# Moving sixteen modulation units into the projection stage, and reordering the attention side work, in a two-block transformer kernel

## The chip, the cores and the metric

The kernel runs on one core of one Trainium2 chip. The time is the device time in microseconds (us) of one launch. Three runs of the kernel before gave 1226.17, 1227.54 and 1229.17 us, median 1227.54 us.

TensorE (PE) multiplies, VectorE (DVE) and ScalarE (ACT) do elementwise work, GpSimd (POOL) computes a few powers, and SyncE (SP) issues most DMAs. Each engine works through its own instruction list in order and waits on semaphores for the others.

## The reference, cut to what matters

One sequence of 256 tokens of width 1024 goes through two blocks, all in fp32.

```python
# block 1
mods = silu(c) @ w_ada + b_ada            # 9 vectors of 1024: shift, scale, gate for 3 sublayers
n = modulate(rmsnorm(h, g_pre0), shift0, scale0);  f = swiglu(n, gate, up, down)   # ffn0
h = h + 0.5 * gate0 * rmsnorm(f, g_post0)
n = modulate(rmsnorm(h, g_pre1), shift1, scale1);  p = n @ w_in
oa = rmsnorm(dsa_sparse_attention(...))   # 8 heads, top 64 keys by an index score, softmax
ob = rmsnorm(stick_breaking_attention(...))   # 8 heads
h = h + gate1 * rmsnorm(concat(oa, ob) @ w_out, g_post1)
n = modulate(rmsnorm(h, g_pre2), shift2, scale2);  f = swiglu(...)                 # ffn1
h = h + 0.5 * gate2 * rmsnorm(f, g_post2)
# block 2
h = h + diff_attention(rms_norm(h), w_qkv, w_o, ...)   # rope on q and k, two softmaxes a head
h = h + sq_relu_mlp(...);  h = h + mla_attention(...);  h = h + sq_relu_mlp(...)
return rms_norm(h)
```

`mods` holds nine vectors, numbered 0 to 8. Vectors 0 and 1 are wanted by ffn0, 2 by the residual after it, 3 and 4 by the projection `w_in`, 5 by the residual after `w_out`, 6 and 7 by ffn1, and 8 by the residual after that.

## The kernel before, in words

**The stream.** All weights lie in DRAM as one stream of units, each 128 x 1024 fp32 (512 KB), in the order that `stream_plan` writes (line 67). SP loads them two at a time (a chunk of 1 MB) into a ring of five chunks, `raw`. `feed` (line 338) takes the units in order. A weight unit is split into two parts that add up to it: ACT copies the high part (`whi`, L354) and DVE subtracts it (`wlo`, L355), into one of five slots, so that PE can multiply with three passes (high x high, high x low, low x high, L392). An "ada" unit is no weight for PE: DVE multiplies it by `silu(c)` and sums it into one column of `mods` (L333), and eight ada units make one of the nine vectors. `spread` (line 69) mixes ada units among weight units; its last argument sets how densely.

**ffn0.** It has 22 blocks of 128 hidden columns. Eight are made while the first modulation vectors arrive, the other 14 pairs (gate, up) and 22 down units follow, 50 weight units, and 48 ada units (vectors 2 to 7) are spread among them. Beside them `constants_and_table` (line 905) advances one step with each pair or down unit: ACT writes a small row table to DRAM (`bias_rows`) and loads it back shifted, 1 MB (`arena<-bias_rows`), and PE flips it in four matmuls (L405), two of them first. `modulations` turns finished vectors into columns and gate rows.

**The projection with attention beside it.** After `in_v` (8 units) and `in_i`, 20 `in_t` units in `IN_ORDER` make the transposed queries and keys. A `Side` object (line 175) runs generators between them: its clock `now` goes up by one with each `nudge`, half way and at the end of each unit, and a part that yields n is resumed n nudges later (2 if it yields nothing). `index_part` scores and picks keys (L1061, L1063 on DVE), `stick_head` and `sparse_head` are the heads. A stick head is: scores on PE; ACT Abs, Exp, Ln and DVE L1108; yield 3; cumulative sums on PE ("second product"), ACT, DVE L1116, ACT L1118; yield 3; times values on PE. A sparse head is: scores; DVE L1084 and L1015, ACT exponentials L1020, DVE L1089; yield 3; transpose (PE L993, ACT L996); yield; times values and DVE L1026. `half_out` normalises eight finished heads (ACT L1175, POOL, DVE L519) and `mixed` multiplies them by the diagonal (PE L1186) into four chunks (ACT L1191, DVE L1192). These are the input of the `out` units, 8 of them in `OUT_ORDER` (chunks 4 to 7 first).

**Differential attention.** 16 `qk` units are projected (q and k in turn). Each needs a rope: ACT L1265 copies, PE L405 turns it, DVE L1270 and L1274 or L1276 add. `rope_end`, put at the head of the side's list by `soon`, does the PE and DVE half at the next nudge, which is half way through the next unit. `diff_head` is the head's generator (DVE L1015, L1320 to L1328, L1342).

## Time and profile before

| what | value |
|---|---|
| median of three runs | 1227.54 us (1226.17 to 1229.17) |
| the profiled execution's own time | 1227.54 us |
| its span | 1226.2 us, mean granted clock 0.985 |
| PE busy | 1171.4 us (96%) |
| DVE busy | 796.8 us (65%) |
| ACT busy | 618.6 us (50%) |
| stream loads on SP | 213 chunks of 1 MB |

The busy share of PE says that some 55 us of the span at most are idle, but it counts a slow matmul as busy too. TensorE's granted clock is 1.00 (2.4 GHz) in most of the span and 0.50 (1.2 GHz) in a few stretches of some 6 us. So time can be lost in two ways, as idle time and as work at half the clock.

### The profile page before, as it was taken

What the parts mean: (1) busy time and instruction counts of PE and PEld (TensorE: products, weight loads), DVE (VectorE), ACT (ScalarE), POOL (GpSimd) and SP (SyncE); (2) the same over time, 40 slices, a digit from 0 to 9 for tenths busy, and PEclk for the clock granted to TensorE, in tenths of its full rate; (3) what the DMA queues carried; (4) which work ended last, traced back from release to release, by engine and by line L of the source; (5) the groups of instructions that cost most, each with busy time, mean ns of one, the idle gap of its engine ahead of it and who ended that gap; (6) DMA issues with size and microseconds to landing.
All of it is one profiled execution on the core that took longest, in us unless ns stands there. A gap on an engine that the chain in (4) does not pass through costs nothing.

```text
span 1226.2 us, 19544 instructions
## 1 busy us (share of the span) xinstructions
PE 1171.4 (96%) x7742; PEld 1074.6 (88%) x7742; DVE 796.8 (65%) x1310; ACT 618.6 (50%) x1114; POOL 55.8 (5%) x75
## 2 busy tenths in 40 slices
PE   4999999999988999999999899999999889999998
PEld 4988799899977999999989788999998778899997
DVE  4879788758654666565667776555557665655554
ACT  5644343646654644444545455554546545555453
POOL 3100000000000000000002110000000100000000
PEclk9999899999998999999999989999999999999999
DMA  8969999443222365654343223545454414554540
GB/s 348 401 261 415 352 344 348 154 180 138 104 98 75 124 240 207 224 218 172 138 176 138 83 104 127 200 175 197 181 190 151 175 35 154 175 200 176 194 150 35
DMA packets 34010, 231.78 MB, mean 189 GB/s; under 512 B 3704, under 2 KB 5120, under 8 KB 6528
## 3 DMA queue, kind: packets, MB, share of 16 engines
q1 hardware_dynamic: 31952, 226.24, 49.9%
q10 hardware_dynamic: 1968, 4.29, 1.0%
q8 instruction: 62, 1.02, 0.3%
q14 instruction: 28, 0.23, 0.1%
HBM read 229.45 MB, written 1.06 MB: 188 GB/s over the span
## 4 chain that ended last, share of the span: by engine, by line
PE 78%; DVE 11%; ACT 5%; issue 2%; DMA 2%; POOL 1%; ACTq 0%; DVEq 0%; SPq 0%; POOLq 0%
PE ps L392 35%; PE pacc L392 34%; DVE wlo L355 3%; PE ps L402 2%; PE ps L405 2%; ACT wk L1020 2%; PE pacc L402 2%; DVE raw L333 1%; DMA raw<-in_stream 1%; ACT whi L354 1%; POOL st L499 1%; PE ps L531 1%; PE pacc L531 1%; DVE st L1015 1%; DVE tmp L668 1%
## 5 line engine op out<-in xcount | busy, mean ns | idle before, releaser
L355 DVE TENSOR_TENSOR wlo<-raw,whi 128x1024 fp32r<-128x1024 f32 x353 | 430.6, 1226 | 194.8 <-ACT whi L354 188.0
L354 ACT ACTIVATE whi<-raw 128x1024 fp32r<-128x1024 f32 x353 | 368.4, 1054 | 164.8 <-PE pacc L392 84.2
L392 PE MATMUL ps<-nhi,whi 128*128 128x256 f32 x1272 | 368.3, 290 | 1.8 <-DVE arena L1270 1.0
L392 PE MATMUL ps<-nlo,whi 128*128 128x256 f32 x1272 | 361.9, 284 | 0.0
L392 PE MATMUL ps<-nhi,wlo 128*128 128x256 f32 x1272 | 361.7, 284 | 0.0
L392 PEld LDWEIGHTS ps<-nhi,whi 128*128 128x128 f32 x1272 | 245.9, 193 | 7.3 <-DVE arena L1270 1.3
L392 PEld LDWEIGHTS ps<-nlo,whi 128*128 128x128 f32 x1272 | 245.9, 193 | 4.9 <-issue 0.8
L392 PEld LDWEIGHTS ps<-nhi,wlo 128*128 128x128 f32 x1272 | 245.7, 193 | 0.0
L743 ACT ACTIVATE sg<-ps 128x256 f32<-128x256 f32 x104 | 39.8, 383 | 164.5 <-PE ps L392 164.3
L392 PE MATMUL pacc<-whi,mhi 128*128 128x512 f32 x240 | 96.5, 402 | 2.4 <-DVE mlo L1192 2.4
L392 PE MATMUL pacc<-wlo,mhi 128*128 128x512 f32 x240 | 94.5, 394 | 0.0
L392 PE MATMUL pacc<-whi,mlo 128*128 128x512 f32 x240 | 93.9, 391 | 0.0
L745 DVE TENSOR_TENSOR hm<-sg,ps 128x256 f32<-128x256 f32 x104 | 43.7, 421 | 69.8 <-ACT sg L743 69.7
L333 DVE SCALAR_TENSOR_TENSOR raw<-raw,silu_c 128x1024 f32<-128x1024 f32 x72 | 88.2, 1233 | 0.3 <-DMA raw<-in_stream 0.3
L392 PE MATMUL pacc<-whi,hhi 128*128 128x512 f32 x188 | 74.4, 396 | 1.8 <-ACT sg L743 1.1
L392 PE MATMUL pacc<-wlo,hhi 128*128 128x512 f32 x188 | 73.6, 392 | 0.0
L392 PE MATMUL pacc<-whi,hlo 128*128 128x512 f32 x188 | 73.2, 389 | 0.0
L499 POOL TENSOR_TENSOR st<-st,mod 128x1 f32<-128x1 f32 (+1 forms) x40 | 26.9, 672 | 1015.7 <-DVE st L689 421.8
L392 PEld LDWEIGHTS pacc<-whi,mhi 128*128 128x128 f32 x240 | 45.7, 190 | 10.9 <-ACT hhi L1191 2.6
L392 PEld LDWEIGHTS pacc<-whi,mlo 128*128 128x128 f32 x240 | 45.4, 189 | 10.1
L392 PEld LDWEIGHTS pacc<-wlo,mhi 128*128 128x128 f32 x240 | 45.7, 191 | 7.8 <-issue 0.5
L392 PE MATMUL pacc<-whi,nhi 128*128 128x512 f32 (+1 forms) x128 | 50.0, 391 | 0.9 <-DVE n2lo L557 0.5
(305 smaller groups left out, 1784.8 us busy)
## 6 DMA issues: line engine op xcount, KB each, us to landing
raw<-in_stream SPq DMA_DIRECT2D x213, 1024.0 KB, 4.9
gates<-in_g_post ACTq DMA_DIRECT2D x3, 512.0 KB, 6.4
h<-in_x SPq DMA_DIRECT2D x1, 1024.0 KB, 7.0
cst<-in_const ACTq DMA_DIRECT2D x1, 1024.0 KB, 4.8
arena<-bias_rows ACTq DMA_DIRECT2D x1, 1024.0 KB, 18.8
out<-tmp SPq DMA_DIRECT2D x4, 256.0 KB, 2.1
silu_c<-in_c_row ACTq DMA_DIRECT2D x1, 512.0 KB, 5.9
arena<-in_final_g SPq DMA_DIRECT2D x1, 512.0 KB, 5.7
```

What stands on the lines that cost most here:

```text
L333: t = dve.do(lambda e: e.scalar_tensor_tensor(src, src, 1.0, silu_c[:, :], ALU.mult, ALU.mult, accum_out=adac[:, 8 * m + k:8 * m + k + 1]) ...
L354: t_hi = act.do(lambda e: e.activation(whi[:, s, :], src, ACT.Copy), arrived, room)
L355: t_lo = dve.do(lambda e: e.tensor_tensor(wlo[:, s, :], src, whi[:, s, :].bitcast(F32), ALU.subtract), arrived, room, t_hi)
L392: return e.matmul(o, lt[a], rh[b], start=start and first, stop=stop and last)
L402: pe.quiet(lambda e: e.matmul(o, lt, rh, start=start, stop=stop), *after)
L405: return pe.do(lambda e: e.matmul(o, lt, rh, start=start, stop=True), *after)
L499: return pool.do(lambda e: e.tensor_tensor(r, v, ex, ALU.pow), t, t_zero)
L531: tok[c] = pe.do(lambda e: e.matmul(o, a, dg[:, i, :], start=True, stop=True), t, held[c].free)
L668: t = dve.do(lambda e: e.scalar_tensor_tensor(tmp[:, i, w], fix[2 * i + f].ap, r1[i], gates[:, slot, w], ALU.mult, ALU.mult), t1[i], t_gate)
L743: t = act.do(lambda e: e.activation(sg[:, m, :], up if gate is None else gate, ACT.Relu if gate is None else ACT.Silu), tk)
L745: t = dve.do(lambda e: e.tensor_tensor(hm[:, m, :], sg[:, m, :], up, ALU.mult), t)
L1020: toks.append(act.do(lambda e: e.activation(dst.ap[:, a:a + w], src[:, a:a + w], ACT.Exp, bias=mx[:, i:i + 1], accum_out=sm[:, i:i + 1]), ...
```

## The change

1. **The stream.** Vectors 6 and 7 (16 ada units) leave ffn0's stretch and are spread among the last ten `in_t` units and the first four `out` units. The 32 units that stay in ffn0 are spread with 1.1 in place of 1.03.
2. **The side work of the projection.** `sparse_head` waits two nudges in place of three between its softmax and its transposes. The sparse heads stand ahead of both `half_out` parts in the list of waiting work. `mixed` is a generator that yields between its four chunks.
3. **Differential attention.** A unit's rope is finished at the end of the next unit, not half way through it, and a head starts three nudges after its k rope or later. `soon` goes.

```diff
-    plan += spread(ffn("ffn0_", DFF // P, ("gate", "up"), 8), (2, 3, 4, 5, 6, 7), 1.03)
+    plan += spread(ffn("ffn0_", DFF // P, ("gate", "up"), 8), (2, 3, 4, 5), 1.1)
     plan += [("in_v", k) for k in range(8)] + [("in_i", 0)]
-    plan += [("in_t", j) for j in IN_ORDER]
-    plan += [("out", k) for k in OUT_ORDER]
+    plan += [("in_t", j) for j in IN_ORDER[0:10]]
+    plan += spread([("in_t", j) for j in IN_ORDER[10:]] + [("out", k) for k in OUT_ORDER[0:4]], (6, 7), 1.2)
+    plan += [("out", k) for k in OUT_ORDER[4:]]
...
-    def soon(self, part):
-
-        self.active.insert(0, (self.now + 1, part))
...
             t_rs = dve.do(lambda e: e.reciprocal(rs, sm), t_e)
-            yield 3
+            yield
             pt, t = transpose_p(lg, t_e)
...
         def mixed(a, chunk, ts):
             for c in range(4):
+                if c:
+                    yield 1
                 b = banks.take()
...
             yield 3
-            mixed(a, chunk, ts)
-            yield
+            yield from mixed(a, chunk, ts)
...
+        for hh in range(8):
+            side.add(sparse_head(hh), lambda hh=hh: ripe(hh // 2, 4 + hh // 2) and sel_at and side.now >= sel_at[0] + 3)
         side.add(half_out(512, 4, t_b, 4096), lambda: len(t_b) == 8 and len(t_sel) == 2)
         side.add(half_out(0, 0, t_a, 5120), lambda: len(t_a) == 8 and 7 in o1.t)
-        for hh in range(8):
-            side.add(sparse_head(hh), lambda hh=hh: ripe(hh // 2, 4 + hh // 2) and sel_at and side.now >= sel_at[0] + 3)
...
-            side.add(diff_head(hh), lambda hh=hh: ripe(hh, 8 + hh))
-
-        def rope_end(at, rope):
-            t_q[at], born[at] = next(rope), side.now
-            yield
-
+            side.add(diff_head(hh), lambda hh=hh: ripe(hh, 8 + hh) and side.now - born[8 + hh] >= 3)
+        pend = None
         for hh in range(8):
             for g in (0, 8):
...
                 next(rope)
+                if pend is not None:
+                    t_q[pend[0]], born[pend[0]] = next(pend[1]), side.now
+                pend = (g + hh, rope)
                 feed()
                 side.nudge()
-                side.soon(rope_end(g + hh, rope))
+
+        def last_rope(at, rope):
+            t_q[at], born[at] = next(rope), side.now
+            yield
+
+        side.add(last_rope(*pend))
```

What stands on the engines follows from the plan and the side's clock. The changed kernel's line numbers are three lower from line 197 to `mixed`, so that L355 before is L352 after and L333 is L330; from `mixed` to the sparse heads' place they are one lower.

On DVE in ffn0, behind the eighth block that was made ahead: the last rows before the ninth block's `hm` (L745), before the change.

```order
L355 TENSOR_TENSOR wlo<-raw,whi 128x1024
L333 SCALAR_TENSOR_TENSOR raw,adac<-raw,silu_c 128x1024
L355 TENSOR_TENSOR wlo<-raw,whi 128x1024
L333 SCALAR_TENSOR_TENSOR raw,adac<-raw,silu_c 128x1024
L745 TENSOR_TENSOR hm<-sg,ps 128x256
```

The same place after it.

```order
L352 TENSOR_TENSOR wlo<-raw,whi 128x1024
L330 SCALAR_TENSOR_TENSOR raw,adac<-raw,silu_c 128x1024
L352 TENSOR_TENSOR wlo<-raw,whi 128x1024 x2
L330 SCALAR_TENSOR_TENSOR raw,adac<-raw,silu_c 128x1024
L742 TENSOR_TENSOR hm<-sg,ps 128x256
```

Five weights and five ada units stand ahead of that `hm` before, five weights and three ada units after; ahead of the tenth `hm` stand four and four more before, four and three after.

On DVE in the projection stage, around the first two stick heads' L1116 (`wk<-wk,pacc`), with the key selection (L1061, L1063) between, before.

```order
L974 TENSOR_SCALAR arena<-ps 64x256
L355 TENSOR_TENSOR wlo<-raw,whi 128x1024
L1116 TENSOR_TENSOR wk<-wk,pacc 128x384
L1061 MAX st<-hm 128x8 x2
L1063 MATCH_REPLACE hm<-st,hm 128x128
L1063 MATCH_REPLACE hm<-st,hm 128x256
L1116 TENSOR_TENSOR wk<-wk,pacc 128x384
```

After.

```order
L971 TENSOR_SCALAR arena<-ps 64x256
L352 TENSOR_TENSOR wlo<-raw,whi 128x1024
L330 SCALAR_TENSOR_TENSOR raw,adac<-raw,silu_c 128x1024 x2
L1113 TENSOR_TENSOR wk<-wk,pacc 128x384
L1058 MAX st<-hm 128x8 x2
L1060 MATCH_REPLACE hm<-st,hm 128x128
L1060 MATCH_REPLACE hm<-st,hm 128x256
L1113 TENSOR_TENSOR wk<-wk,pacc 128x384
```

Two ada units stand between a weight and the heads' work here, and one or two behind each of eleven other weights of the stage.

On DVE ahead of the first chunk that `out` needs (L1192, `mlo`), behind the diagonals of the stick half (L519), before.

```order
L519 TENSOR_SCALAR dg<-cst,st 128x128
L974 TENSOR_SCALAR arena<-ps 64x256
L355 TENSOR_TENSOR wlo<-raw,whi 128x1024
L1026 TENSOR_SCALAR tmp<-pacc,st 128x64 x2
L1084 TENSOR_TENSOR wk<-ps,arena 128x128
L1084 TENSOR_TENSOR wk<-ps,arena 128x256
L1015 TENSOR_REDUCE st<-wk 128x1 x2
L1089 RECIPROCAL st<-st 128x2
L1026 TENSOR_SCALAR tmp<-ps,st 128x64 x2
```

After, at the same place, the rows up to that chunk.

```order
L516 TENSOR_SCALAR dg<-cst,st 128x128
L352 TENSOR_TENSOR wlo<-raw,whi 128x1024
L1081 TENSOR_TENSOR wk<-ps,arena 128x128
L1081 TENSOR_TENSOR wk<-ps,arena 128x256
L1012 TENSOR_REDUCE st<-wk 128x1 x2
L1086 RECIPROCAL st<-st 128x2
L1081 TENSOR_TENSOR wk<-ps,arena 128x128
L1081 TENSOR_TENSOR wk<-ps,arena 128x256
L1012 TENSOR_REDUCE st<-wk 128x1 x2
L1086 RECIPROCAL st<-st 128x2
```

Before, one more such softmax and a weight follow the rows shown and then the chunk's L1192. After, two rows of L1026 follow and then L1192. The diagonals themselves stand behind the sixth sparse head's softmax now, and before they stood ahead of the fifth's.

## Rows read from the trace of the kernel before

**Rows 1.** The page, part 1: busy us (share) x instructions by engine.

```profile
PE 1171.4 (96%) x7742; PEld 1074.6 (88%) x7742; DVE 796.8 (65%) x1310; ACT 618.6 (50%) x1114; POOL 55.8 (5%) x75
```

**Rows 2.** Stretches: us from:to, length, busy by engine, granted clock, DMA share, GB/s.

```profile
128.30:135.00 6.70, 6.69 (x27) 5.66 (x28) 5.71 (x9) 1.17 (x2) 0.00 (x0) 0.54 1.01 419
290.00:314.00 24.00, 23.99 (x185) 23.22 (x184) 20.65 (x63) 16.31 (x34) 0.00 (x0) 1.00 0.36 129
314.00:357.00 43.00, 43.00 (x346) 42.31 (x345) 25.20 (x56) 26.62 (x66) 1.10 (x2) 1.00 0.29 101
357.00:364.70 7.70, 2.51 (x18) 1.96 (x17) 4.02 (x13) 4.64 (x14) 0.00 (x0) 0.90 0.00 1
363.60:370.00 6.40, 5.32 (x15) 4.43 (x16) 2.25 (x6) 0.81 (x2) 0.00 (x0) 0.50 0.45 166
387.40:393.10 5.70, 5.43 (x20) 4.95 (x21) 3.28 (x6) 1.90 (x4) 0.00 (x0) 0.50 0.52 184
640.00:715.00 75.00, 69.09 (x493) 65.19 (x493) 57.54 (x137) 36.17 (x108) 14.95 (x20) 0.95 0.29 102
```

**Rows 3.** PE in order of time, at the table: start, length, instruction [idle before].

```profile
128.31 1.22 PE L405 MATMUL ps<-arena,cst 128*128 128x512 f32 x1 [2.96 <-DVE wlo L355]
```

**Rows 4.** ACT in order of time, the two DMAs of the table.

```profile
102.25 0.42 ACT L751 ACTIVATE hhi<-hm 128x256 fp32r<-128x256 f32 x1 [3.93 <-DVE hm L745]
...
104.97 0.56 ACTq L136 DMA_DIRECT2D bias_rows<-wk  x1
...
109.42 0.42 ACTq L136 DMA_DIRECT2D arena<-bias_rows  x1
```

**Rows 5.** DMA from 90 to 135: packets, MB, share; issue, KB, us to landing.

```profile
q1 hardware_dynamic: 2422, 17.65, 94.5%
q10 hardware_dynamic: 1056, 1.06, 6.9%
...
arena<-bias_rows ACTq DMA_DIRECT2D x1, 1024.0 KB, 18.8
```

**Rows 6.** DVE in order of time in ffn0.

```profile
99.52 1.22 DVE L355 TENSOR_TENSOR wlo<-raw,whi 128x1024 fp32r<-128x1024 f32 x1
100.66 1.22 DVE L333 SCALAR_TENSOR_TENSOR raw<-raw,silu_c 128x1024 f32<-128x1024 f32 x1
...
101.80 0.42 DVE L745 TENSOR_TENSOR hm<-sg,ps 128x256 f32<-128x256 f32 x1
```

**Rows 7.** DVE in order of time, three operations of the stick heads.

```profile
300.35 0.56 DVE L1116 TENSOR_TENSOR wk<-wk,pacc 128x384 f32<-128x384 f32 x1
...
306.77 0.55 DVE L1108 SCALAR_TENSOR_TENSOR wk<-ps,wk 128x384 f32<-128x384 f32 x1
...
315.86 0.56 DVE L1108 SCALAR_TENSOR_TENSOR wk<-ps,wk 128x384 f32<-128x384 f32 x1 [0.19 <-ACT wk L1107]
```

**Rows 8.** PE in order of time, what uses them, and a transpose.

```profile
303.04 0.56 PE L402 MATMUL ps<-arena,wk 128*128 128x64 f32 x4
...
308.08 0.71 PE L402 MATMUL pacc<-wk,cst 128*128 128x256 f32 x3
...
318.76 0.71 PE L402 MATMUL pacc<-wk,cst 128*128 128x256 f32 x3
...
329.32 0.49 PE L993 MATMUL pacc<-cst,wk 128*128 128x128 f32 x3
```

**Rows 9.** ACT in order of time, the end of the second sparse head's softmax.

```profile
328.76 0.19 ACT L1020 ACTIVATION_READ_ACCUMULATOR wk<-wk,st 128x1 f32 x1
```

**Rows 10.** PE in order of time, the two waits around `out`.

```profile
364.69 0.76 PE L392 MATMUL pacc<-whi,mhi 128*128 128x512 f32 x1 [2.40 <-DVE mlo L1192]
...
386.65 0.49 PE L1186 MATMUL ps<-dg,tmp 128*128 128x128 f32 x2 [2.54 <-DVE st L505]
387.67 1.22 PE L1186 MATMUL ps<-dg,tmp 128*128 128x128 f32 x4 [0.53 <-DVE dg L519]
```

**Rows 11.** DVE in order of time, one weight in each of two differential heads.

```profile
690.18 1.23 DVE L355 TENSOR_TENSOR wlo<-raw,whi 128x1024 fp32r<-128x1024 f32 x1
...
701.16 1.23 DVE L355 TENSOR_TENSOR wlo<-raw,whi 128x1024 fp32r<-128x1024 f32 x1
```

## The prediction, on record before the change was run

> **What bounds the kernel now.** I read the page's busy shares first. PE is busy for 96% of the span [rows 1], so the kernel is bound by PE, and only what makes PE idle or slow can be won or lost. DVE and ACT matter where PE waits for them. Next I read the stretches, where the reader is to look for two things, PE's busy time under the length of the stretch, and a granted clock of 0.50, the lower of the two levels (1.2 GHz against 2.4 GHz). The change touches three stages, and each has such a place.
>
> In ffn0, PE stands still for 2.96 us ahead of 128.31 [rows 3]. The row names a weight's low part, but the instruction that then starts is the flip of the table. The table's load was issued at 109.42 and took 18.8 us [rows 4, 5], which is 128.2, so it is the load that ends the wait. Behind it PE runs 6.70 us at a clock of 0.54 [rows 2], which loses 6.70 x 0.46 = 3.1 us. Together 6.1 us hang on when that load lands.
>
> In the projection with `out`, PE is full up to 357 (43.00 of 43.00 us) [rows 2]. Then come 7.7 us with 2.51 us of work, 5.2 us lost, and 5.32 us of work at half the clock, 2.7 us lost [rows 2]. The second wait is 2.54 + 0.53 = 3.1 us [rows 10], with 5.43 us of work at half the clock behind it, another 2.7 us [rows 2]. These are 13.7 us in all.
>
> In differential attention PE has 69.09 us of work in 75 us [rows 2]. DVE starts the same weight of two successive heads at 690.18 and 701.16 [rows 11], a period of 10.98 us. I followed DVE through one period, and nothing in it waits for PE, only for ACT and POOL. So DVE sets the pace there.
>
> **Part one, ffn0.** A weight's low part takes DVE 1.14 us from start to start (99.52 to 100.66) and an ada unit 1.14 us (100.66 to 101.80) [rows 6]. PE reaches the table when its own products are done (128.31 - 2.96 = 125.35 [rows 3]), whatever DVE does, since the same products stand ahead of it. What moves is the issue of the load. ACT came to the small write at 104.97 [rows 4] because it had waited 3.93 us for the tenth block's `hm` until 102.25 [rows 4], and DVE reached that at 101.80 [rows 6] behind its queue. The change takes two ada units from ahead of the ninth `hm` and one from ahead of the tenth, 3 x 1.14 = 3.4 us. So the write goes out about 3.5 us earlier, and the load with it, at 105.9. With 18.8 us [rows 5] it lands at 124.7, ahead of 125.35. I take the whole wait and the slow stretch as gone, -6.1 us. The bounds are 0 (the load is still late by enough to drop the clock) and -6.5 (two smaller waits of PE early in the stage go too). The other ada units that leave ffn0 give nothing, since PE is full from 135 on. What DVE saves there was hidden behind PE.
>
> The load's price is more open than its start. In the trace the stream's queue has 2422 packets for 17.65 MB and the table's queue 1056 packets for 1.06 MB [rows 5]. So a table packet has 1 KB and a stream packet some 7 to 8 KB. The Trainium skill ("DMA: Bandwidth & Descriptors", Queues, rings and completion order) says that each DMA engine takes turns between the queues it has work for, a packet at a time. By that rule 1056 / 16 = 66 table packets on each engine wait for about as many stream packets, and 45 us x 16 x 0.945 / 2422 = 0.28 us each makes 18.5 us, and the trace agrees (18.8). By that rule a thinner stream does not shorten the load as long as the ring of five chunks is not full, and only the earlier start counts. If the load shared by bytes instead, the thinner stream (82 units in place of 98 for the same PE work) would bring it down by about 18.8 x 16 / 98 = 3 us, and the term would be as safe as its start. The sum is the same by both, -6.1 us.
>
> **Part two, the projection.** Sixteen ada units of 1.14 us [rows 6] come to DVE, 18.3 us. From 290 to 314 DVE is busy for 20.65 of 24.00 us, and from 314 to 357 for 25.20 of 43.00 [rows 2]. On average there is room. In the first of these stretches there is hardly any. I count up DVE's delay where PE uses its result, by order rows and start times.
>
> Four ada units stand ahead of the first stick head's L1116, 4.6 us, and DVE had only 0.2 us of idle time since the first of them. L1116 began at 300.35 [rows 7] and ends near 305.1 now, ACT's exponential follows until 305.7, and PE wants it at 303.04 [rows 8]. PE is 2.7 us late. A fifth unit, and the rest of the idle time, bring L1108 of the third stick head from 306.77 [rows 7] to 312.5. PE wants it at 308.08 [rows 8], so PE is 4.5 us late in all. L1108 of the sixth stick head (315.86 [rows 7], wanted at 318.76 [rows 8]) gives 6.2 us in all. It follows two more ada units, and ACT, which must do the fourth head's logarithms behind the delayed L1116, passes the delay on.
>
> Then come the sparse heads with one nudge less. The second one's softmax ends at 328.76 + 0.19 = 328.95 [rows 9] and PE transposes at 329.32 [rows 8], so there were 0.4 us to spare. Now PE comes to it one half unit and some head work earlier, about 2.1 us, and an ada unit of 1.14 us stands between the two softmaxes, so the wait is 3 us by itself. Carried on from 6.2, the first transpose makes it 8.3 and the second 11.7. The third and fourth heads repeat this pattern and I get 15.5. The sixth adds 1.4 and the diagonals 0.9.
>
> At the end of the stage `out` waits for its first chunk. DVE reaches the diagonals only behind the sixth softmax, and two more softmaxes, each with a wait for ACT, stand between them and L1192. I get a wait of 6.3 us where 5.2 us were lost before. Two new short waits follow, since a chunk is made right ahead of the products that use it, 1.2 + 1.1 us. The clock falls once, and much of its fall lies in the wait, 1.8 us. What goes is the wait of 3.1 us at 386.65 and its 2.7 us of slow clock. The norm of the sparse half now has 24 products of `out` (5.5 us) ahead of it, more than the 3.5 us that it took.
>
> The sum is 15.5 + 1.4 + 0.9 + 6.3 + 2.3 + 1.8 = 28.2 us against 13.7, +14.5. When I write out the start times one after the other instead, `out` ends 10 us later than before. The two ways differ since in the second I count PE's own steps a little short, and since waits overlap. I take +12, between them. Here are the bounds. All of the 16 units go into idle time of DVE, and only the second wait goes, -5.8. At the upper end the two waits of 3.4 us at the transposes also bring the clock down, as 2.96 us did [rows 3], and cost 3 us more, +17.
>
> **Part three, the rope.** PE's turn of the rope moves half a unit (1.44 us) later. DVE used it 1.1 us or more after PE had it, and the DVE list is the same but for one pair of rows. DVE's period stays, so the waits of PE only change place, 0 us. Bounds from both sides, -1.5 and +1.5, half a unit either way.
>
> **The sum.** -6.1 + 12 + 0 = +5.9 us. The profiled execution took 1227.54 us (span 1226.2), and this is also the median, so I predict 1233.4 us.
>
> **The rivals.**
> 1. *DVE's idle time takes the moved units (faster).* What speaks for it is 25.20 of 43.00 us busy [rows 2], and that side work is spaced to be late without harm. What speaks against it is 0.4 us to spare at the transpose and a full DVE around 300. Its price would be +4 in the first stretch, and -5.8 with the second wait, and a first wait no longer than before: 1227.5 - 6.1 + 4 - 5.8 = 1219.6 us. Chance 0.23. It decides if PE's waits up to 357 sum to under 6 us.
> 2. *The load still lands late (slower yet).* If the small write is not earlier by 3 us, the flip waits still and the clock falls: 1227.5 + 12 = 1239.5 us. For it speaks that the margin is only 0.6 us. Chance 0.15.
> 3. *The two parts cancel.* With the projection at +6, half of what I count, the time is 1227.4 us. This happens if the waits of PE give DVE more time than I allow. Chance 0.12.
> 4. *The change doesn't do what it says.* This holds for part three, where DVE's list is the same. It is in the forecast.
>
> The forecast has a chance of 0.50, with its own range 1230 to 1238 us.
>
> **How the numbers follow.** About 0.2% (2.5 us) is what a measurement of this kernel can tell from no change. Faster: rival 1 and a part of rival 3, 0.26. Same: most of rival 3 and the lower edge of the forecast, 0.11. Slower: the forecast and rival 2, 0.63. The range from 1219.5 to 1240 us leaves out some 0.1 on each side.
>
> **What would show it.** Right: no idle time of PE over 1 us and a clock of 1.00 in the stretch around 125 to 135; PE idle for 2 us or more at the first stick head's times-values product, and for about 3 us at the second and fourth sparse heads' transposes; DVE nearly full from 290 to 330; one wait of 5 us or more at the first `out` product, and none at the sparse half's first chunk; a period of 11.0 us in differential attention. Wrong: PE full from 290 to 357 as before, which is rival 1, or a flip that still waits, which is rival 2.

## The result

The changed kernel takes 1243.78 us (median of 4 runs, 1240.43 to 1244.54) against 1228.36 us for the kernel before (median of 4 runs, 1226.17 to 1229.34). The ratio is 1.0122, with a 95% interval of [1.0098, 1.0147]. It is slower, as forecast, but by 15 us where 5.9 were forecast, and 3.8 us above the range. The profiled execution's span is 1240.7 us against 1226.2, 14.5 us more.

The page, part 1, of the changed kernel (busy us, share, instructions), beside [rows 1]:

```profile
PE 1173.0 (95%) x7742; PEld 1075.5 (87%) x7742; DVE 798.7 (64%) x1310; ACT 620.2 (50%) x1114; POOL 56.4 (5%) x75
```

PE is busy for only 1.6 us more. The other 12.9 us are idle time, 67.7 us in place of 54.8. DVE's busy time and its 1310 instructions are the same. The loss is in where the work stands.

Stretches of the changed kernel: around the table's flip, the projection from the first stick head to the end of `out`, and the four stretches of it with a slow clock. The columns are those of [rows 2].

```profile
125.00:132.00 7.00, 7.00 (x51) 6.33 (x50) 5.24 (x7) 2.61 (x3) 0.00 (x0) 1.00 0.84 302
284.76:416.68 131.92, 108.54 (x704) 99.78 (x703) 84.73 (x200) 62.88 (x145) 2.75 (x5) 0.94 0.41 149
334.00:338.00 4.00, 3.19 (x17) 3.22 (x17) 2.17 (x5) 2.99 (x10) 0.00 (x0) 0.57 0.43 176
361.00:365.00 4.00, 4.00 (x22) 4.00 (x22) 1.70 (x3) 1.80 (x5) 0.00 (x0) 0.57 0.16 41
375.00:379.00 4.00, 3.90 (x16) 3.54 (x16) 2.92 (x8) 1.71 (x5) 0.55 (x1) 0.57 0.16 23
382.00:389.00 7.00, 5.72 (x19) 4.96 (x19) 1.41 (x6) 0.95 (x4) 0.00 (x0) 0.51 0.01 2
```

The same stretch of the kernel before, and its two slow ones.

```profile
289.97:403.15 113.18, 104.91 (x702) 97.39 (x701) 65.78 (x165) 62.30 (x144) 2.75 (x5) 0.94 0.28 97
...
363.00:370.00 7.00, 5.32 (x15) 4.43 (x16) 2.85 (x6) 1.41 (x4) 0.00 (x0) 0.51 0.42 153
387.00:394.00 7.00, 6.47 (x24) 5.66 (x23) 3.35 (x6) 1.92 (x5) 0.29 (x1) 0.51 0.42 150
```

The projection grew by 131.92 - 113.18 = 18.7 us. Idle time of PE went from 113.18 - 104.91 = 8.3 us to 131.92 - 108.54 = 23.4 us, +15.1. A slow stretch costs its busy time times what the clock lacks of 1.00: 3.19 x 0.43 + 4.00 x 0.43 + 3.90 x 0.43 + 5.72 x 0.49 = 7.6 us against 5.32 x 0.49 + 6.47 x 0.49 = 5.8 us, +1.8. The last 1.8 us are busy time of PE at the full clock. Most of it comes out of the way the records count. Ahead of most waits matmuls start 0.11 to 0.12 us apart, but each record is 0.27 to 0.28 us long, so the last one ahead of a wait sticks out by some 0.16 us. The changed kernel has 14 waits in the stretch and the kernel before has 5, and 9 x 0.16 makes 1.4 us. What is left is 0.4 us.

DVE is busy for 84.73 of 131.92 us, 64%. Such a mean looks harmless, and PE waits all the same. PE of the changed kernel in order of time, all its waits over 0.8 us in the projection (start, length, instruction [idle before]), to be read against [rows 8, 10]:

```profile
294.29 0.92 PE L399 MATMUL pacc<-wk,cst 128*128 128x256 f32 x4 [0.85 <-DVE wk L1105]
...
300.61 0.66 PE L399 MATMUL ps<-arena,wk 128*128 128x64 f32 x4 [1.49 <-ACT wk L1115]
...
307.61 0.70 PE L399 MATMUL pacc<-wk,cst 128*128 128x256 f32 x2 [1.71 <-DVE wk L1105]
...
319.98 0.48 PE L399 MATMUL pacc<-wk,cst 128*128 128x256 f32 x1 [0.99 <-DVE wk L1105]
...
328.97 0.52 PE L990 MATMUL ps<-cst,wk 128*128 128x128 f32 x3 [1.79 <-ACT wk L1017]
...
334.81 0.88 PE L990 MATMUL ps<-cst,wk 128*128 128x128 f32 x3 [3.27 <-ACT wk L1017]
...
354.65 0.52 PE L990 MATMUL pacc<-cst,wk 128*128 128x128 f32 x3 [0.98 <-ACT wk L1017]
...
360.59 0.52 PE L990 MATMUL pacc<-cst,wk 128*128 128x128 f32 x3 [3.38 <-ACT wk L1017]
...
373.28 0.52 PE L990 MATMUL ps<-cst,wk 128*128 128x128 f32 x3 [1.55 <-ACT wk L1017]
375.10 0.69 PE L399 MATMUL ps<-arena 128*128 128x128 f32 x2 [1.13 <-ACT arena L1219]
...
383.28 0.77 PE L389 MATMUL pacc<-whi,mhi 128*128 128x512 f32 x1 [3.66 <-DVE mlo L1191]
...
391.79 0.47 PE L389 MATMUL pacc<-whi,mhi 128*128 128x512 f32 x1 [1.18 <-DVE mlo L1191]
...
404.15 0.47 PE L389 MATMUL pacc<-whi,nhi 128*128 128x512 f32 x1 [1.18 <-DVE nlo L1191]
```

DVE ahead of the second of these waits, where L1113 answers to L1116 of [rows 7]:

```profile
295.90 1.23 DVE L352 TENSOR_TENSOR wlo<-raw,whi 128x1024 fp32r<-128x1024 f32 x1
297.04 1.22 DVE L330 SCALAR_TENSOR_TENSOR raw<-raw,silu_c 128x1024 f32<-128x1024 f32 x1
...
298.18 1.22 DVE L330 SCALAR_TENSOR_TENSOR raw<-raw,silu_c 128x1024 f32<-128x1024 f32 x1
...
299.44 0.56 DVE L1113 TENSOR_TENSOR wk<-wk,pacc 128x384 f32<-128x384 f32 x1
```

Two ada units, 2.3 us, stand right ahead of L1113, and PE waits for ACT's L1115, which follows it.

At the table the gain came as forecast. ACT at the two DMAs, beside [rows 4]; then the load from issue to landing, beside [rows 5]; then the flip, beside [rows 3].

```profile
99.16 0.42 ACT L748 ACTIVATE hhi<-hm 128x256 fp32r<-128x256 f32 x1 [2.60 <-DVE hm L742]
101.88 0.53 ACTq L137 DMA_DIRECT2D bias_rows<-wk  x1
106.32 0.41 ACTq L137 DMA_DIRECT2D arena<-bias_rows  x1
```

```profile
arena<-bias_rows ACTq DMA_DIRECT2D x1, 1024.0 KB, 13.1
```

```profile
126.01 1.02 PE L402 MATMUL ps<-arena,cst 128*128 128x512 f32 x2
```

The load was issued 3.1 us earlier, and it was also 5.7 us shorter. It landed at 119.4, far ahead of the flip, which has no wait, and the clock is 1.00 there. `in_v` begins at 230.09 in place of 237.10. Of these 7.0 us, 2.0 only changed place: 16 matmuls for a gate's rows stood in ffn0 before and stand in `in_v` now, as PE's row shows.

```profile
232.93 1.95 PE L625 MATMUL ps<-cst,mod 128*128 128x128 f32 x16
```

Differential attention took about 1 us more (138.65 us from the residual behind ffn1 to the residual behind `o_a`, against 137.56). DVE's period is as in [rows 11], 10.99 us, and PE's waits stand at the heads' transposes now. DVE first, then PE.

```profile
681.65 1.23 DVE L352 TENSOR_TENSOR wlo<-raw,whi 128x1024 fp32r<-128x1024 f32 x1
...
692.64 1.23 DVE L352 TENSOR_TENSOR wlo<-raw,whi 128x1024 fp32r<-128x1024 f32 x1
```

```profile
698.68 0.52 PE L990 MATMUL pacc<-cst,wk 128*128 128x128 f32 x3 [1.20 <-DVE wk L1326]
```

### The profile page after: what moved, and what is told of

The parts are those of the page before. It is cut to its first block, busy times and chain, and to the rows that moved or that the text cites. A ratio compares the mean times of both kernels' runs of the same rounds, so it can differ in the third digit from the quotient of the medians.

```text
span 1240.7 us, 19536 instructions
## 1 busy us (share of the span) xinstructions
PE 1173.0 (95%) x7742; PEld 1075.5 (87%) x7742; DVE 798.7 (64%) x1310; ACT 620.2 (50%) x1114; POOL 56.4 (5%) x75
## 4 chain that ended last, share of the span: by engine, by line
PE 77%; DVE 12%; ACT 6%; issue 2%; DMA 1%; POOL 1%; DVEq 0%; SPq 0%; ACTq 0%; POOLq 0%
PE ps L389 35%; PE pacc L389 34%; DVE wlo L352 3%; ACT wk L1017 2%; PE ps L399 2%; DVE raw L330 1%; ACT whi L351 1%; PE ps L402 1%; PE pacc L399 1%; PE ps L528 1%; DVE st L1012 1%; PE pacc L528 1%; POOL st L496 1%; DVE tmp L665 1%; DMA raw<-in_stream 1%
## 5 line engine op out<-in xcount | busy, mean ns | idle before, releaser
L352 DVE TENSOR_TENSOR wlo<-raw,whi 128x1024 fp32r<-128x1024 f32 x353 | 430.6, 1226 | 191.2 <-ACT whi L351 183.5
L389 PE MATMUL ps<-nhi,whi 128*128 128x256 f32 x1264 | 363.3, 287 | 2.5 <-DVE arena L1268 1.7
L330 DVE SCALAR_TENSOR_TENSOR raw<-raw,silu_c 128x1024 f32<-128x1024 f32 x72 | 87.4, 1226 | 0.0
```

What stands on the lines that cost most here:

```text
L330: t = dve.do(lambda e: e.scalar_tensor_tensor(src, src, 1.0, silu_c[:, :], ALU.mult, ALU.mult, accum_out=adac[:, 8 * m + k:8 * m + k + 1]) ...
L352: t_lo = dve.do(lambda e: e.tensor_tensor(wlo[:, s, :], src, whi[:, s, :].bitcast(F32), ALU.subtract), arrived, room, t_hi)
L389: return e.matmul(o, lt[a], rh[b], start=start and first, stop=stop and last)
```

## The experiments

The table is for all of them. Ratios are to the kernel before, which was run again beside each group of experiments. The stage runs from the first matmul of the residual behind ffn0 (PE L531 of the kernel before) to that of the residual behind `out`, in the profiled execution, and so holds the 2.0 us that changed place. In e3, e5 and e9 a few records at an end of the stage are missing, so their lengths are good to half a us.

| kernel | median us | ratio, 95% interval | stage us | first `out` product after us |
|---|---|---|---|---|
| before | 1226.97 to 1228.36 | 1 | 175.95 | 131.7 |
| changed | 1243.78 | 1.0122 [1.0098, 1.0147] | 196.33 | 157.3 |
| e1 plan alone | 1235.97 | 1.0070 [1.0055, 1.0084] | 191.96 | 148.9 |
| e2 side work alone | 1231.34 | 1.0033 [1.0020, 1.0047] | 179.28 | 140.1 |
| e3 rope alone | 1229.54 | 1.0013 [1.0002, 1.0023] | 176 | |
| e4 units early | 1223.50 | 0.9970 [0.9958, 0.9982] | 177.29 | 135.0 |
| e5 DVE's part left out | 1224.75 | 0.9973 [0.9963, 0.9982] | 181.5 | 142.2 |
| e6 third nudge back | 1242.00 | 1.0117 [1.0100, 1.0133] | 196.00 | 153.8 |
| e7 three waits filled | 1240.94 | 1.0098 [1.0081, 1.0114] | 198.30 | 159.5 |
| e8 all units late in ffn0 | 1230.23 | 1.0023 [1.0010, 1.0035] | 176.03 | 133.3 |
| e9 load later | 1243.20 | 1.0126 [1.0102, 1.0150] | 198 | 159.2 |
| e10 units among `out` | 1235.64 | 1.0062 [1.0047, 1.0076] | 192.71 | 149.3 |
| e11 evener plan | 1221.62 | 0.9951 [0.9936, 0.9967] | 175.36 | 132.9 |
| e12 e11 with fillers | 1223.79 | 0.9966 [0.9946, 0.9986] | 177.14 | 136.9 |
| e13 all long waits filled | 1236.20 | 1.0085 [1.0065, 1.0105] | 192.53 | 156.2 |
| e14 e11, fillers in own bank | 1225.45 | 0.9995 [0.9979, 1.0012] | 180.12 | 139.2 |

The theory was that DVE's time for the moved units delays what PE waits for, and that the clock falls behind the waits. The rivals were that the new side order costs, that the denser stream costs, or that the table's load does.

**e1, e2, e3: each part alone.** Each kernel is the one before with a part of the diff above: e1 the plan's lines, e2 `yield` for `yield 3`, `mixed` in steps and the sparse heads ahead, e3 the lines of differential attention.

> The kernel before with the stream's new plan alone: ffn0 keeps 32 ada units, 16 go among in_t and out; the side work and the rope stay as they were. Theory A (the moved ada units delay DVE, DVE delays PE, and each wait of PE also brings the granted clock down): ffn0 -7.0 and in_v +1.8 as in the changed kernel, and the stage from the first stick head to the end of out most of its +18.7, about +10 to +15, less some for the third nudge of slack that the sparse heads keep. 1227.5 - 7 + 1.8 + 12 = 1234 us. Rival B (the reordered side work is what costs, the ada units go into idle time of DVE): the stage grows by 0 to 3, and the time is 1222 to 1225 us.

> The kernel before with the projection's new side work alone: two nudges in place of three before the transposes, sparse heads ahead of half_out, mixed in four steps; plan and rope as before. Theory A: little by itself, since DVE has its idle time: transposes late by 1.5 to 3 us in all, the first wait at out a little longer, the second wait (3.1 us and 2.7 us of slow clock) gone. 1227 to 1231 us. Rival B (this edit holds most of the cost): 1235 us or more. A third possibility, that it pays (the second wait goes and nothing comes in its place): 1222 us.

> The kernel before with differential attention's new rope order alone. In the changed kernel this stage took 0.9 us more. By that: 1228.4 us, within 1 us either way. If the extra came from elsewhere (a shifted phase of the stream), it is exactly as before.

The plan alone costs 16.0 us in the stage and gives 7.1 ahead of it. The side work alone costs 3.3 in the stage, and the rope 0.9 between the residual behind ffn1 and the residual behind `o_a`. One pair of executions doesn't show 0.9 us: the nine kernels with the old rope order take 136.9 to 138.6 us there, the seven with the new one 138.2 to 138.9. The means differ by 0.8. 16.0 + 3.3 = 19.3 of the changed kernel's +20.4, so the parts nearly add, and rival B of e1 falls. The ratios add as well, 0.0070 + 0.0033 + 0.0013 = 0.0116 against 0.0122. Which of its three edits makes the cost of the side work was not tried one by one, but for the nudge (e6). e1 and e2 came out some 2 and 0.3 us above their ranges. In e1 PE waits before transposes as long as in the changed kernel, though the sparse heads kept their third nudge, and at the diagonals' chunk:

```profile
334.70 0.87 PE L994 MATMUL pacc<-cst,wk 128*128 128x128 f32 x3 [3.83 <-ACT wk L1021]
...
359.12 0.87 PE L994 MATMUL ps<-cst,wk 128*128 128x128 f32 x3 [3.05 <-ACT wk L1021]
...
374.69 0.47 PE L393 MATMUL pacc<-whi,mhi 128*128 128x512 f32 x1 [2.05 <-DVE mlo L1193]
```

e2's profiled execution had a longer load of the table (23.2 us), in a part that it shares with the kernel before. PE waited 5.80 us there, not 2.96. e3 has that part too, and its load took 19.9 us. That is the spread of one and the same code.

```profile
131.79 1.22 PE L405 MATMUL ps<-arena,cst 128*128 128x512 f32 x1 [5.80 <-DMA arena<-bias_rows]
```

**e5: DVE's time alone.** The edit to the changed kernel:

```diff
+            n = 8 if m in (6, 7) else D
-            t = dve.do(lambda e: e.scalar_tensor_tensor(src, src, 1.0, silu_c[:, :], ALU.mult, ALU.mult,
+            t = dve.do(lambda e: e.scalar_tensor_tensor(src[:, 0:n], src[:, 0:n], 1.0, silu_c[:, 0:n], ALU.mult, ALU.mult,
```

> The changed kernel, but of the ada units of vectors 6 and 7 DVE sums only the first 8 of 1024 columns, so that each takes a small part of its 1.14 us; the stream and its order stay the same. Theory A (DVE's time is what the moved units cost): the projection falls back to what the side work alone costs, about +3.3 over before in place of +18.7, and with ffn0 (-7 and +1.8) and the rope (+0.9) the time is 1226.5 us. Rival C (the denser stream or the ring of chunks delays the weights): it stays near 1243 us.

The stream is the changed kernel's (168 GB/s in this shorter stretch, 149 there), DVE has 84.7 - 69.3 = 15.4 us less to do, and the ratio is lower by 0.0149, 18.3 us. The stretch from the first stick head to the end of `out`, and the first wait that is left:

```profile
284.70:402.00 117.30, 105.81 (x719) 98.43 (x717) 69.34 (x208) 64.37 (x147) 2.75 (x5) 0.96 0.46 168
```

```profile
325.61 0.52 PE L991 MATMUL ps<-cst,wk 128*128 128x128 f32 x3 [1.43 <-ACT wk L1018]
```

No wait over 0.4 us stands ahead of 325 any more, and none of 3 us at a transpose. That DVE's time is the cause is shown, and rival C is out.

**e6: the nudge.** The changed kernel with `yield 3` for `yield` ahead of `transpose_p`.

> The changed kernel with three nudges again between a sparse head's softmax and its transposes. Theory A (the nudge is a small part, since DVE's delay is carried on from one head to the next and only moves from one wait to another): 1 to 3 us less, 1241 to 1243 us. Rival D (the nudge is what the waits of 3.3 us at the second and fourth transpose hang on): their 6.6 us and 3.1 us of slow clock go, 1234 us.

By the ratio it makes no difference that can be told. The waits at the transposes are 3.83 and 3.05 us, as in e1, and the one ahead of the first `out` product grew from 3.66 to 6.04 us. What is not waited for early is waited for late, since DVE is behind.

**e4, e8, e11: other places for the units.** The edits are to the plan of the kernel before, e4, e8 and e11 in this order. e8 keeps the `in_v` line as it was.

```diff
+    plan += spread(units[:12], (2,), 1.05) + spread(units[12:], (3, 4, 5, 6), 1.03)
+    plan += spread([("in_v", k) for k in range(8)] + [("in_i", 0)], (7,), 1.15)
...
+    plan += spread(units[:12], (2,), 1.05) + spread(units[12:], (3, 4, 5, 6, 7), 1.03)
...
+    plan += spread(units[:20], (2, 3), 0.92) + spread(units[20:], (4, 5, 6), 1.1)
+    plan += spread([("in_v", k) for k in range(8)] + [("in_i", 0)], (7,), 1.15)
```

> The kernel before with another plan: in ffn0 only vector 2 is spread among the first 12 weight units, vectors 3 to 6 among the other 38, and vector 7 among in_v and in_i, where DVE is busy for some 34 of 53 us; nothing is added beside the heads. Theory A (the gain of ffn0 comes from few ada units ahead of the table's load, the loss from ada units beside the heads): ffn0 -6 to -7, in_v 0 to +1, the stage with out as before: 1221.5 us. Rival (the load lands sooner only because the stream is thinner up to 125 us, and a denser stream behind it or a DVE fuller in in_v gives the gain back): 1225 to 1228 us.

> The kernel before with another order of ffn0's stream alone: vector 2 among the first 12 weight units, vectors 3 to 7 among the other 38, so that all 48 ada units stay in ffn0 but three fewer stand ahead of the table's load. Theory A (the table needs few ada units ahead of its load, and PE hides them behind it): the wait and the slow stretch at the table go, nothing else changes, 1221.5 us. Rival: 40 ada units among 38 weights fill DVE in the rest of ffn0 and PE waits there, or the load takes 19 us or more again with a thick stream: 1225 us or more.

> The kernel before with vectors 2 and 3 among ffn0's first 20 weight units, 4 to 6 among the other 30, and 7 among in_v and in_i; side work and rope as before. Theory A: as e4, with an evener DVE at ffn0's end: the load of the table in a pause of the stream, no wait at the flip, 1222 to 1223.5 us. Rival: the stretch in which the stream pauses moves off the load (as with 40 units behind the first 12, where the load took 24.6 us), 1228 us.

e11 beats both kernels, 0.5% under the one before. It keeps the gain at the table and adds nothing beside the heads. e4 lands between its theory and its rival: it reaches the stage 4.8 us earlier, and the stage is 1.3 us longer. e8 is a miss that teaches: its load was issued at 104.67, 4.8 us earlier than before, and PE still waited.

```profile
104.67 0.41 ACTq L137 DMA_DIRECT2D arena<-bias_rows  x1
```

```profile
arena<-bias_rows ACTq DMA_DIRECT2D x1, 1024.0 KB, 24.6
```

```profile
129.27 1.22 PE L406 MATMUL ps<-arena,cst 128*128 128x512 f32 x1 [4.70 <-DMA arena<-bias_rows]
```

With 40 ada units behind the first 12 weights the load took 24.6 us. With 32 (e4) it took 12.0. So an earlier start is not enough where the load itself gets longer. But it is enough where the load stays as long as before, and e11 shows that. Its load took 19.6 us and was issued 3.8 us earlier than in the kernel before, and it landed at 125.25, just ahead of the flip, which has no wait:

```profile
105.65 0.41 ACTq L137 DMA_DIRECT2D arena<-bias_rows  x1
```

```profile
arena<-bias_rows ACTq DMA_DIRECT2D x1, 1024.0 KB, 19.6
```

```profile
125.34 1.12 PE L406 MATMUL ps<-arena,cst 128*128 128x512 f32 x2
```

The loads of e12 and e14, with the plan of e11, took 20.0 and 19.7 us, and PE waited for 0.20 us and not at all.

**e9: the load, later.** The edit is to the changed kernel:

```diff
-            yield
+            for _ in range(3):
+                yield
             t_staged = act.load(staged ...
-            for _ in range(6):
+            for _ in range(4):
```

> The changed kernel, but the table's load is issued two steps (a pair and a down unit) later, near 115 us in place of 106.3, with the flip at the same step as before. In the changed kernel's trace the load ran fast in one stretch only, from 110 to 113 us, where the stream's queue had 54 packets in place of some 170 in 3 us. Theory F (the load lands early when the stream pauses while it runs, and else at the pace of one table packet for one stream packet): the pause at 110 is missed, the load takes 15 us or more, lands at 130 or later, and PE waits for 4 us or more with a slow stretch behind, so 1248 to 1251 us. Rival G (a thinner stream makes every load short, 12 to 13 us): it lands at 127 to 128, PE waits 2 to 3 us: 1245 to 1249 us, and the load's time tells them apart.

Both theories missed. The issue moved by 3.4 us only, to 109.70 (the steps were shorter than I took them), the load took 14.8 us, and PE did not wait. The stretch in which the table moves fast went along with the issue, so it is not a pause of the stream that happens to be there. Queues in three us where the load runs about fastest: e9 from 113 to 116, then the changed kernel from 110 to 113, then the kernel before from 115 to 118 (q10 is the table, q1 the stream: packets, MB, share).

```profile
q10 hardware_dynamic: 789, 0.80, 82.8%
q1 hardware_dynamic: 41, 0.32, 27.7%
```

```profile
q10 hardware_dynamic: 792, 0.81, 82.3%
q1 hardware_dynamic: 54, 0.31, 26.2%
```

```profile
q1 hardware_dynamic: 111, 0.78, 65.2%
q10 hardware_dynamic: 383, 0.39, 38.1%
```

The fast stretch doesn't set the landing, though. e9 has as fast a stretch as the changed kernel and its load is 1.7 us longer. In e11 the last packets take the time, here those from 116 us to the landing:

```profile
q10 hardware_dynamic: 52, 0.05, 1.6%
```

So 52 packets took nine us there, beside a stream at full pace. Why the last ones are slow no run shows.

**e10: the units among `out`.** The plan of ffn0 is the changed kernel's (vectors 2 to 5, 1.1). What is left of `modulations` for vectors 6 and 7 is done ahead of the residual behind `out`.

```diff
-    plan += [("out", k) for k in OUT_ORDER]
+    plan += spread([("out", k) for k in OUT_ORDER], (6, 7), 1.3)
...
+        while todo[0][0] <= 7:
+            modulations(True)
```

> The kernel before with vectors 6 and 7 moved out of ffn0 as in the change, but put among the eight out units alone, none beside in_t, and the side work and rope as before. Theory A (a moved unit costs only where DVE's result is waited for by PE soon): ffn0 -5, the stage up to the first out product as before, and of the 18.3 us of DVE's work most in its idle 23 us of the out stage, with the residual late by 0 to 4 us: 1222 to 1227 us. Rival: the units delay the norm of the sparse half (its L505 and L519, for which PE waits 2.5 us already) and each waits on through out: 1230 us or more.

It went the rival's way, but not at the rival's place. The longest wait stands ahead of `out`, at a transpose, and the next at the first chunk.

```profile
349.46 0.87 PE L993 MATMUL ps<-cst,wk 128*128 128x128 f32 x3 [5.39 <-ACT wk L1020]
...
373.62 0.76 PE L392 MATMUL pacc<-whi,mhi 128*128 128x512 f32 x1 [4.97 <-DVE mlo L1192]
```

`feed` runs ahead by five slots, and it does all ada units that it meets on its way. So a unit placed among `out` is DVE's work five weights earlier, beside the last sparse heads: the first of the 16 runs at 334.5 us, 39 us ahead of the first `out` product.

**e7, e13: the clock.** e7 puts `busy(26)` ahead of two transposes and `busy(30)` ahead of `rows_times`; e13 is the changed kernel with these lines:

```diff
             yield
+            if hh in (0, 1, 3, 5):
+                busy(26 if hh in (1, 3) else 13)
             pt, t = transpose_p(lg, t_e)
...
+                if chunk == 4 and c == 0:
+                    busy(30)
                 k = chunk + c
```

> The changed kernel with matmuls of 128 columns on the identity, whose result nobody uses, put on PE where it waits longest: 26 (3.0 us by 0.114 us for one) ahead of the second and the fourth sparse head's transposes, 30 ahead of the first out product. Nothing else moves. Theory A (each wait brings down the granted clock behind it, and that costs on top of the wait): the falls at 334, 361 and 382 us, 1.4 + 1.7 + 2.8 us lost in the changed kernel, go wholly or in part, 1239 to 1241 us. Rival E (the clock falls whatever stands in the wait): 1243 to 1245 us.

> The changed kernel with matmuls on the identity (0.114 us each) in all of the projection's long waits from 328 us on: 13, 26, 26 and 13 ahead of the transposes of the first, second, fourth and sixth sparse head (waits of 1.79, 3.27, 3.38 and 1.55 us), and 30 between the first diagonal products and the first out product (3.66 us). Theory A (the clock is a price on top of the waits): all four falls of 7.6 us in the stage go, 1236 to 1238 us. Rival E (fillers cost PE time of their own or the falls come later all the same): 1240 us or more.

In e7 the falls at 334 and 361 are gone. The 30 fillers came too early (they stand ahead of the diagonals), the wait of 3.49 us stayed, and the clock fell at 372 and at 382. This profiled execution's stage is no shorter. The ratio is lower by 0.0024, which is within the noise of the two. In e13 the clock is 1.00 from the first stick head to the end of `out`.

```profile
284.00:411.00 127.00, 114.21 (x818) 106.11 (x817) 85.25 (x204) 63.42 (x144) 2.55 (x5) 1.00 0.42 152
```

Its stage is 3.8 us shorter than the changed kernel's. Ahead of the stage's heads, around 260 us, its clock fell for 1.7 us more than there, which is the spread seen in others too, so some 5.5 us come from the fillers. The ratios differ by 0.0037, 4.5 us, with intervals that just overlap. So most of the 7.6 us is a price on top of the waits. The rest may lie in time in which PE would have waited for DVE anyway, which no run shows.

**e12, e14: the same on e11.** The fillers stand around the diagonals in `mixed`, 12 ahead and 20 (18) behind for chunk 4, 20 ahead for chunk 0, in e14 in a bank taken first.

> e11 with matmuls on the identity in PE's waits around out: 12 ahead of the stick half's diagonals (the wait there is 1.56 us), 20 behind them (2.40 us), 20 ahead of the sparse half's diagonals (2.54 us), 0.114 us each. Theory A (the clock falls behind a wait, and filling it keeps the clock up): the two slow stretches of the kernel before at 363 to 370 and 387 to 394 us, 2.7 + 3.2 us lost, go: 3 to 5 us less than e11. Rival E (the fall comes all the same a little later, as it did with the fillers of e7): 0 to 1 us less than e11.

> e11 (the fastest plan) with the fillers of e12 in a PSUM bank that is taken ahead of the diagonals' four, so that the 18 behind them need not wait for one: 12 ahead of the stick half's diagonals, 18 behind them, 20 ahead of the sparse half's. Theory A: the falls of 1.4 and 2.9 us behind these waits go and the fillers lie in the waits: 1217 to 1219 us. Rival E: as e12, no gain over e11 or a loss, 1221 to 1224 us.

Both are misses: no gain over e11, and e14 costs 0.4% against e11. The fall behind the sparse half's diagonals, at 381 us in e11, did go in both. The trouble is in the stick half. In e12 the fillers waited for a bank, and ran when the wait was over. In e14 a wait of 1.96 us stood ahead of the last diagonals, since the fillers held one bank and these had to wait for another (its row names `mlo`, DVE L1205). The clock had fallen, and 18 fillers took 4.1 us at half the clock. First e12, then e14.

```profile
363.01 0.44 PE L406 MATMUL ps<-identr 128*128 128x128 f32 x2 [1.51 <-DVE mlo L1193]
```

```profile
361.00:372.00 11.00, 9.06 (x35) 8.38 (x36) 2.89 (x5) 2.22 (x6) 0.00 (x0) 0.53 0.28 96
```

## Why the prediction was right and wrong

| term | forecast | measured in the profiled executions |
|---|---|---|
| ffn0 | -6.1 | -7.0, and +1.8 in `in_v`: -5.2 |
| projection, waits of PE | +18.1 (26.4 against 8.3) | +15.1 (23.4 against 8.3) |
| projection, slow clock | -3.6 (1.8 against 5.4) | +1.8 (7.6 against 5.8) |
| projection, other busy time of PE | 0 | +1.8 |
| projection, taken | +12 | +18.7 |
| differential attention | 0 | +1.0 |
| sum | +5.9 | +14.5 |

**Right.** The direction, and the mechanism at nearly each place: PE late at the first stick head by 0.85 + 1.49 = 2.3 us (2.7 said), then 1.7 more (1.8), 1.0 (1.7), 1.8 and 3.3 at the first two transposes (2.1 and 3.4), 4.4 at the next two (3.8), 1.6 at the sixth (1.4), and two of 1.2 (1.2 and 1.1).

Three places came out otherwise. The wait at the first `out` product was 3.66 us and not 6.3, and so not the "5 us or more" among the signs. The diagonals were to cost 0.9 and ran without a wait. In their stead PE waited for 1.13 us at 375.10 for ACT's copy of the last key unit (L1219), which the scores of a sparse head need. And the second of the two waits of 1.2, at 404.15, stands at the sparse half's first chunk, where the signs name none.

**Wrong, first step.** "The clock falls once, and much of its fall lies in the wait, 1.8 us." It fell four times and cost 7.6 us. I had the warning in the bounds ("the two waits of 3.4 us at the transposes also bring the clock down") and left it to the upper end. The row of 2.96 us of idle time with 3.1 us of slow clock behind it [rows 2, 3] was near, and the same stage had a wait of 3.1 us with 2.7 us of slow clock behind it [rows 2, 10]. That should have been the value. With the measured 7.6 the sum of the items is 28.2 + 5.8 = 34.0 against 13.7, +20.3, and with the wait at `out` in its true size +17.7.

**Wrong, second step.** "I take +12, between them." The items' sum was +14.5, and the second way was known to count PE's steps short. Averaging with a figure of known bias took 2.5 us off. The two steps make 5.8 + 2.5 = 8.3 us, and the profiled executions differ from the forecast by 8.6. The other misses nearly cancel: waits -3.0, the clock of the kernel before -0.4, other busy time +1.8, ffn0 +0.9, differential attention +1.0.

**Partly right by luck.** The table's load was to gain by its earlier start. It was issued at 106.32, and with the 18.8 us of the kernel before it would have landed at 125.1, ahead of the flip at 126.01. e11 shows that such a start does the work by itself. But the load also got 5.7 us shorter, which the prediction had argued away, and e8 shows that it can get longer as well: 4.8 us earlier, and it landed at 129.3, later than before. So the forecast rested on a load that happened to be no longer than before.

The price of the load was worked out wrongly. The rule of the Trainium skill ("DMA: Bandwidth & Descriptors", Queues, rings and completion order), that each DMA engine takes turns between its queues by the packet, gave 18.5 us. That sum took each packet that the profile counts for one turn, and it left out the time of the table's own packets, 45 us x 16 x 0.069 / 1056 = 0.05 us each, 3.1 us for 66. With them it is 21.6 us, and the trace's 18.8 agrees with 18.5 by luck. One packet for one is not what the traces show either: where the load moved fast there were 383 packets of the table beside 111 of the stream in the kernel before, and 792 beside 54 in the changed kernel. The measurement decides.

What does hold is that the plan sets the load's time. With 32 ada units in ffn0 eight executions took 11.5 to 14.8 us, and with 48 four took 18.8 to 24.6. e10 and e8 issued the load at the same time, 104.72 and 104.67, and it took 13.4 and 24.6 us. How the plan does it is open: from 106 to 125 us the stream moved about the same in both groups, 6.5 to 6.7 MB. Why some executions of one code take 18.8 and others 23.2 us (e2) is open too.

**Small misses.** The gate's rows, 2.0 us, moved from one stage into the next and gave nothing, as the -5.2 shows. The rope's waits did not only change place, the stage grew by 1 us, inside the bound of 1.5. The upper bound of the projection should be 14.5 + 3 = +17.5, not +17, and the measured +18.7 lies above both.

Rival 1 (idle DVE absorbs the units) fell by e5 and e1. Rival 2 (load still late) did not happen in the changed kernel, but did in e8. Rival 3 (the parts cancel) wanted +6 in the projection, which took +18.7. What stays open is what sets the load's time, and what part of a fall of the clock a filler can save, since of four tries with fillers only e13 gained more than the noise.

## What to carry to other kernels

Where two engines alternate, ask for the slack at each handover and not for an engine's mean load: 18 us of DVE work in a stage with 47 us of idle DVE cost 14 us (e1, without the gate's rows), and all 48 units kept ahead of the heads, eight of them beside `in_v`, cost nothing there that shows (e11, a stage of 175.36 us against 175.95). Move such work by where its engine does it, which here is five weights ahead of its place in the plan. Price a wait of PE of 3 us with the slow stretch behind it, about 1.5 to 3 us more, until a trace shows that there is none. Don't take the length of a load from one trace when the plan around it changes. And when two countings of one quantity differ, find the error in one of them rather than take the middle.

## What the runs showed of the hardware

- A load of 1 MB beside a stream took 11.5 to 14.8 us with 32 ada units left to spread in ffn0 and 18.8 to 24.6 us with 48. With 40 it took 12.0 in e4 and 19.6 to 20.0 in e11, e12 and e14. In the kernels with 48 most of the table was there by 122 us, and from then on only 9 to 24 of its queue's packets came in each 3 us until the landing.
- The granted clock fell to 0.50 in or just behind waits of 3.27, 3.38 and 3.66 us, but also behind 1.55 + 1.13 us, and in the kernel before behind 2.40 and 2.54 + 0.53 us.
- It also fell once in every kernel between 256 and 273 us, where PE did not wait at all. What PE did there just before the fall, or still did at it, is the matmuls of `in_i`, 48 of 72 columns each that start 0.11 us apart (from 258.98 to 264.14 us in the kernel before, where the clock fell at 264.2). It cost 1.7 us in the kernel before, the changed kernel, e1 and e6, and 3.4 us in the others.
- With matmuls on the identity in the waits the clock stayed at 1.00 through 127 us (e13). Placed behind a wait, or made to wait for a bank, they cost what they take (18 of them 4.1 us at half the clock in e14).
